# The front of a transformer-block kernel: five columns of x in exchanged blocks, squares from the blocks, first weights in four groups, rstd transposes inside the last column

## The chip, the cores and the metric

The kernel runs on one core of one Trainium2 chip. The metric is the time of one execution in device microseconds. TensorE is PE here (PEld is its weight load), VectorE DVE, ScalarE ACT, GpSimd POOL, SyncE SP. A line such as L2218 is a line of the kernel before.

## The reference

A whole block of an encoder on x of 1024 x 1024 floats: RMS norm, one combined projection, two kinds of attention, output projection, norm, residual, and a squared-ReLU MLP.

```
def rmsnorm(x, g):
    y = xf * lax.rsqrt(jnp.mean(xf * xf, axis=-1, keepdims=True) + EPS)
    return (y * g.astype(jnp.float32)).astype(x.dtype)
...
    h = rmsnorm(x, g_pre_mix[l])
    proj = jnp.einsum('bsd,de->bse', h, w_in[l]) + b_in[l]
    aq, ak, av, bq, bk, bv = jnp.split(proj, splits, axis=-1)
    out_a = mixer_a(aq, ak, av, sinks[l], t5_bias)
    out_b = mixer_b(bq, bk, bv, rel_table[l])
    y = jnp.einsum('bse,ed->bsd', jnp.concatenate([out_a, out_b], axis=-1), w_out[l])
    x = x + rmsnorm(y, g_post_mix[l])
    u = jnp.square(jax.nn.relu(jnp.einsum('bsd,df->bsf', rmsnorm(x, g_pre_mlp[l]), w_up[l])))
    x = x + rmsnorm(jnp.einsum('bsf,fd->bsd', u, w_down[l]), g_post_mlp[l])
```

The change touches the first norm and the first pieces of the projection only.

## The kernel before, in words

**Number form.** Every operand of a large product is split into a high part rounded to fp32r and a low part, the rest; a product is three matmuls: high by high, high by low, low by high. So each operand costs a rounding copy on ACT (`x_hi`, `w1_hi`, `wv_hi`) and a subtraction on DVE (`x_lo`, `w1_lo`, `wv_lo`).

**The front.** x is taken in eight columns k of 128 features by 1024 rows. The norm's factor g1 is put on with the rounding; the row factor rstd is put on later, on the products. For the projection the features must lie on the partitions, so each column is turned. Columns 0 to 4 are loaded as rows (`xraw`) and turned by PE, eight 128x128 transposes per column into PSUM banks 6 and 7 (`x_transposes`, L2230); there ACT reads them for `x_hi` (L1115) and DVE for `x_lo` (L1542). Columns 5 to 7 (`EXCHANGED`) are loaded by four DMAs each with their 32x32 blocks already in exchanged places (`x_blocks`, L693, in pieces of 128 bytes); a STREAM_TRANSPOSE on DVE, which turns within 32x32 blocks, then gives the column (`x_turned`, L1549). Of a column PE makes the products with three tiles of first weights, e in the order 2, 0, 1, each in two halves of 512 rows, with three matmuls of 128x512 for each: 18 per column, summed in PSUM over the columns (`first_products`, L2218 to L2220).

**The row norm.** ACT squares rows of `xraw` (columns 0 to 4, 128x640, L1090) and of a second copy of columns 5 to 7 as rows (`x_rows`, 128x384, L1092), eight each, and accumulates each over its row; DVE adds the two halves (L1556), ACT takes the root (L1122), DVE makes rstd, DVE and ACT lay it out in columns (`rcols`, L1562, L1126), PE turns these by eight transposes (L2290) ahead of column 7, and ACT copies the result out of PSUM (`rrow`, L1142).

**The value products.** Next PE makes value products for row tiles 0 and 1, over all eight k, two halves each; those of tile 0 wait for rrow and, at each k, for `wv_lo` k (L1521). While they run, DVE scales the first tiles by rrow (`tile_scaled`, L1582), ACT rounds them (L1136), DVE takes their low part (`tile_lo`, L1595).

**What sets the order.** Every engine's program is written out by hand, as loops over k with waits on semaphores; an engine runs its own list strictly in order. Tables shape it: `SQUARED` says behind which column's rounding ACT squares which rows, `SPLIT_WITH` which first weights it rounds there, `VALUES_WITH` which value weights DVE handles between the scaled tiles. All big loads go out on SP's queue in written order. POOL makes bias rows, and then issues nine small loads of constants (L980 to L987) behind a wait for column 6. Two of the waits matter later on: ACT's copy of value weights 5 waits for DVE's scaling of the query biases (`s_bsc`, L1568), and the fill weights on SP's queue (L726) for the last squares.

Of the kernel before, what the change touches and what calls it, by code (L numbers as in the profile page):

```python
# [50 lines left out]
SQUARED = ((), (), (), (0, 1, 2, 3), (4, 5, 6), (7, 8, 9, 10, 11), (12, 13, 14, 15), ())  # L51
# [145 lines left out]
EXCHANGED = (5, 6, 7)  # L197
# [3 lines left out]
SPLIT_WITH = ((), (1,), (2,), (3,), (4, 5), (6, 7), (), ())  # L201
# [4 lines left out]
def column_done(k):  # L206

    return 2 * (k + 1) if k < 2 else k + 3

# [50 lines left out]
def build(nc, x, w_in, b_in, w_out, sinks, t5, rel, g_pre_mix, g_post_mix, g_pre_mlp, g_post_mlp,  # L260
# [11 lines left out]
    with ctx:  # L272
# [32 lines left out]
        x_rows = sb("x_rows", 188, [P, T, KT - KX, P])  # L305
# [4 lines left out]
        sq = sb("sq", 150.25, [P, 2, KX, P])  # L310
        wv_hi = [sb(f"wv_hi{k}", at, [P, VW], F32R) for k, at in enumerate((84, 86.5, 89, 91.5, 94, 96.5, 116, 118.5))]
# [3 lines left out]
        x_blocks = {k: sb(f"x_blocks{k}", at, [P, SEQ]) for k, at in zip(EXCHANGED, (92, 76, 108))}  # L315
        x_turned = {k: sb(f"x_turned{k}", at, [P, SEQ]) for k, at in zip(EXCHANGED, (112, 116, 76))}
# [82 lines left out]
        def blocks_landed(k):  # L399
            return {5: (s_xb, 64), 6: (s_g1, 16 + 64), 7: (s_x0, 16 + 64)}[k]  # L400
# [3 lines left out]

        def load_first_weights(eng, g):
            k0, k1 = ((0, 1), (1, 3), (3, KT))[g]
            eng.dma_start(w1_raw[:, k0:k1, 0:P], w_in[AK, :, k0:k1, :]).then_inc(s_w1[g], 16)
            for hh in range(2):
                if g == 0:
                    eng.dma_start(w1_raw[:, 0, P:3 * P].rearrange("p (a n) -> p a n", a=2)[:, :, 64 * hh:64 * hh + 64],  # L410
                                  w_in[2 * hh, :, 0].rearrange("p (a n) -> p a n", a=2)).then_inc(s_w1[g], 16)
                else:
                    for p in range(2):
                        at = P + P * p + 64 * hh
                        eng.dma_start(w1_raw[:, k0:k1, at:at + 64], w_in[2 * hh, :, k0:k1, 64 * p:64 * p + 64]  # L415
                                      ).then_inc(s_w1[g], 16)
# [89 lines left out]
        s_g1 = sem("g1_landed")  # L506
# [5 lines left out]
        s_id = sem("ones_then_ident_ready")  # L512
# [14 lines left out]
        s_ss1 = sem("sumsq_halves_added")  # L527
# [152 lines left out]
        def _(sp):  # L680
# [2042 lines left out]
```

## Time and profile before

| what | us |
|---|---|
| median of 3 runs | 1035.18 (1034.83 to 1035.95) |
| the profiled execution | 1036.56 |
| its span | 1034.3 |
| PE busy in it | 1023.8 (99%) |
| DVE busy | 765.0 |
| ACT busy | 471.2 |
| POOL busy | 217.6 |

The profiled execution is a single run, 1.38 us above the median of the others; 2.3 us of it lie outside the span. The granted TensorE clock was 0.999 of full speed. A timeline row gives the start in the span, the busy time, engine, line, operation and tile, how many instructions were put together, and, in brackets, how long the engine had been idle before and on what. Starts of neighbouring instructions overlap a little, so the distance between two starts is often under the busy time. A row of windows gives a stretch and its length, then busy time and count of PE, PEld, DVE, ACT and POOL in it, then the granted clock, the busy share of the DMA engines and what they moved.

### The profile page before, as it was taken

To read this page: it belongs to the slowest core of one execution; us is meant where nothing else is said; L and a number is where in the kernel's file an instruction comes from. 1 tells how busy PE (TensorE), PEld (TensorE's weight loads), DVE (VectorE), ACT (ScalarE), POOL (GpSimd) and SP (SyncE) were. 2 spreads that over 40 slices of the span, in tenths; PEclk is the share of its full clock that TensorE was granted. 3 is DMA by queue.
4 is the path that set the end of the run, shared out by engine and by line. 5 is a ranking of instruction groups with operands and counts; after the bars stand their busy time and mean duration, and the time that the engine had idled before them with its cause. 6 is when DMAs were issued, how large, how long until landed. Compare 5 with 4: busy or idle time off the path is not lost.

```text
span 1034.3 us, 15804 instructions
## 1 busy us (share of the span) xinstructions
PE 1023.8 (99%) x5531; PEld 851.2 (82%) x5531; DVE 765.0 (74%) x1498; ACT 471.2 (46%) x989; POOL 217.6 (21%) x213
## 2 busy tenths in 40 slices
PE   8999999999999999999999999999999999999997
PEld 7899887778777888888888888888888888888886
DVE  3854678866689478888988788786454777778997
ACT  5732355554478477846131221221354444444562
POOL 4100000000000003148675675671100000000000
PEclk9999999999999999999999999999999999999999
DMA  9944442110061475145444434446777733454344
GB/s 212 238 130 120 119 130 64 63 49 22 27 202 65 122 174 153 41 132 214 163 173 162 164 132 153 163 141 215 246 244 238 239 98 96 138 196 142 95 138 168
DMA packets 133007, 149.50 MB, mean 145 GB/s; under 512 B 68136, under 2 KB 83376, under 8 KB 130880
## 3 DMA queue, kind: packets, MB, share of 16 engines
q1 hardware_dynamic: 131856, 148.25, 46.3%
q8 instruction: 45, 0.74, 0.3%
q14 instruction: 34, 0.28, 0.1%
q10 hardware_dynamic: 688, 0.20, 0.1%
q0 software_dynamic: 384, 0.04, 0.1%
HBM read 105.22 MB, written 47.49 MB: 148 GB/s over the span
## 4 chain that ended last, share of the span: by engine, by line
PE 94%; SPq 3%; issue 1%; DVE 1%; ACT 1%; DMA 0%; DVEq 0%; ACTq 0%
PE ps L2218 27%; PE ps L2220 27%; PE ps L2219 27%; PE ps L2431 3%; PE ps L2417 3%; PE ps L2398 2%; SPq L693 1%; PE ps L2342 1%; PE ps L2377 1%; PE ps L2550 1%; PE ps L2552 1%; PE ps L2538 1%; SPq L415 1%; PE ps L2568 0%; SPq L684 0%
## 5 line engine op out<-in xcount | busy, mean ns | idle before, releaser
L2219 PE MATMUL ps<-tm_lo,sm_hi 128*128 128x512 f32 (+1 forms) x450 | 174.6, 388 | 0.0
L2220 PE MATMUL ps<-tm_hi,sm_lo 128*128 128x512 f32 (+1 forms) x450 | 174.6, 388 | 0.0
L2218 PE MATMUL ps<-tm_hi,sm_hi 128*128 128x512 f32 (+1 forms) x450 | 174.6, 388 | 0.0
L2218 PE MATMUL ps<-b_hi,wc_hi 128*128 128x512 f32 x448 | 174.6, 390 | 0.0
L2220 PE MATMUL ps<-b_hi,wc_lo 128*128 128x512 f32 x448 | 174.3, 389 | 0.0
L2219 PE MATMUL ps<-b_lo,wc_hi 128*128 128x512 f32 x448 | 174.3, 389 | 0.0
L1475 ACT ACTIVATE sm_hi<-sm_raw 128x512 fp32r<-128x512 f32 x112 | 70.7, 631 | 162.1 <-DMA sm_raw<-u_matrices 162.1
L2122 DVE TENSOR_TENSOR sm_lo<-sm_raw,sm_hi 128x512 fp32r<-128x512 f32 x112 | 77.5, 692 | 78.4 <-ACT sm_hi L1475 77.7
L2219 PEld LDWEIGHTS ps<-tm_lo,sm_hi 128*128 128x128 f32 x450 | 84.5, 188 | 17.6
L2218 PEld LDWEIGHTS ps<-tm_hi,sm_hi 128*128 128x128 f32 x450 | 84.5, 188 | 17.4
L2218 PEld LDWEIGHTS ps<-b_hi,wc_hi 128*128 128x128 f32 x448 | 84.1, 188 | 17.8 <-DVE wc_lo L1894 0.3
L2220 PEld LDWEIGHTS ps<-tm_hi,sm_lo 128*128 128x128 f32 x450 | 84.5, 188 | 17.3
L2220 PEld LDWEIGHTS ps<-b_hi,wc_lo 128*128 128x128 f32 x448 | 84.1, 188 | 17.7
L2219 PEld LDWEIGHTS ps<-b_lo,wc_hi 128*128 128x128 f32 x448 | 84.1, 188 | 17.2
L1387 ACT ACTIVATE p1s<-ps 128x512 f32<-128x512 f32 x16 | 9.6, 598 | 181.1 <-PE ps L2220 175.5
L2124 DVE TENSOR_TENSOR tm_lo<-w,tm_hi 128x512 fp32r<-128x512 f32 x112 | 76.6, 684 | 0.0
L1894 DVE TENSOR_TENSOR wc_lo<-up_raw,wc_hi 128x512 fp32r<-128x512 f32 x48 | 56.6, 1202 | 19.6 <-ACT wc_hi L1327 19.6
L1894 DVE TENSOR_TENSOR wc_lo<-wc_raw,wc_hi 128x512 fp32r<-128x512 f32 x64 | 68.9, 1079 | 2.5 <-POOL wc_raw L1036 2.5
L1484 ACT ACTIVATE tm_hi<-w 128x512 fp32r<-128x512 f32 x112 | 69.0, 616 | 0.0
L1028 POOL TENSOR_TENSOR wc_raw<-up_raw 128x512 f32<-128x512 f32 x16 | 22.4, 1401 | 221.4 <-DVE small L673 138.6
L2218 PE MATMUL ps<-x_hi,wf_hi 128*128 128x512 f32 x160 | 66.7, 417 | 0.0
L2220 PE MATMUL ps<-x_hi,wf_lo 128*128 128x512 f32 x160 | 62.8, 392 | 0.0
(256 smaller groups left out, 2057.5 us busy)
## 6 DMA issues: line engine op xcount, KB each, us to landing
u_matrices<-stage SPq DMA_DIRECT2D x112, 256.0 KB, 2.0
sm_raw<-u_matrices SPq DMA_DIRECT2D x112, 256.0 KB, 2.7
up_raw<-in_w_up SPq DMA_DIRECT2D x16, 1024.0 KB, 5.1
w<-in_w_down SPq DMA_DIRECT2D x64, 256.0 KB, 4.2
w_raw<-in_w_in SPq DMA_DIRECT2D x8, 512.0 KB, 3.5
xr<-in_x SPq DMA_DIRECT2D x8, 512.0 KB, 4.8
x_rows<-xr SPq DMA_DIRECT2D x8, 512.0 KB, 5.5
xf<-x_rows SPq DMA_DIRECT2D x8, 512.0 KB, 3.6
```

The costliest lines, as they stand in the source:

```text
L1028: nc.gpsimd.tensor_tensor(wc_raw[s][5][:], a21, a22, ALU.add).then_inc(s_wsum, 1)
L1475: nc.scalar.activation(sm_hi[r][:], sm_raw[r][:], ACT.Copy).then_inc(s_shi, 1)
L1484: nc.scalar.activation(tm_hi[r][:], down_weights[q][c][:], ACT.Copy).then_inc(s_thi, 1)
L1894: nc.vector.tensor_tensor(wc_lo[s][p][:], src, wc_hi[s][p][:].bitcast(F32), ALU.subtract).then_inc(s_wlo[s], 1)
L2122: nc.vector.tensor_tensor(sm_lo[r][:], sm_raw[r][:], sm_hi[r][:].bitcast(F32), ALU.subtract).then_inc(s_slo, 1)
L2124: nc.vector.tensor_tensor(tm_lo[r][:], down_weights[q][c][:], tm_hi[r][:].bitcast(F32), ALU.subtract).then_inc(s_tlo, 1)
L2218: pe.matmul(out, w_hi_, x_hi_, start=start, stop=False)
L2219: pe.matmul(out, w_hi_, x_lo_, start=False, stop=False)
L2220: return pe.matmul(out, w_lo_, x_hi_, start=False, stop=stop)
L2398: last = pe.matmul(score_of(n, hh)[:, c * width:(c + 1) * width], q[rows, tok], k[rows, keys], start=(i == 0), stop=(i == 2))
L2417: last = pe.transpose(ps[:, bank, i * P:(i + 1) * P], prob_of(n, hh)[:, c0 + k * P:c0 + (k + 1) * P], ident[:])
L2431: last = pe.matmul(ps[64 * hh:64 * hh + 64, 7, (t % 4) * P:(t % 4) * P + P], v_tok[:, t + 1 - nk + k, at + 64 * hh:at + 64 * hh + 64], pro ...
```

## The change

- Columns 3 and 4 are now loaded as exchanged blocks too and turned by DVE; PE turns columns 0 to 2 only. `x_rows` is gone.
- The squares of columns 0 to 2 come from rows as before (eight of 128x384). Those of columns 3 to 7 are taken by ACT on the blocks (`square_blocks`, 128x1024 each) into three buffers. POOL adds those of columns 4, 5 and 6 to those of 3. DVE sums that buffer and the squares of column 7 over the 32 elements of each block (`tensor_reduce`), adds both, PE adds over the partitions with a matrix `sel` of zeros and ones (`add_squares`, 128x32, behind e = 2 of column 6), and DVE puts the result on `ss1` in four small additions.
- The first weights come in four groups instead of three; SP waits for the first x_hi and x_lo before the last of them.
- The row transposes stand behind e = 2 of column 7 instead of ahead of column 7.
- In DVE's list the order at columns 3 to 7 is different, ACT's value copies 0 and 1 stand ahead of the root, and DVE's scaling of the query biases stands behind the first two scaled tiles.
- POOL's nine small loads stand behind its additions instead of behind a wait for column 6.

The diff, cut to its core:

```diff
-SQUARED = ((), (), (), (0, 1, 2, 3), (4, 5, 6), (7, 8, 9, 10, 11), (12, 13, 14, 15), ())
+SQUARED = ((), (), (0, 1, 2, 3, 4, 5), (6, 7), (), (), (), ())
...
-EXCHANGED = (5, 6, 7)
+FIRST_GROUPS = ((0, 1), (1, 3), (3, 5), (5, KT))
+EXCHANGED = (3, 4, 5, 6, 7)
...
-SPLIT_WITH = ((), (1,), (2,), (3,), (4, 5), (6, 7), (), ())
+SPLIT_WITH = ((), (1,), (2,), (3, 4), (5,), (6,), (7,), ())
...
+def blocks_squared(k):
+    return rows_squared(k) + k - EXCHANGED[0] + 1
...
-            load_x(0)
...
-            load_x_blocks(7)
+            for k in range(KT):
+                if k in EXCHANGED:
+                    load_x_blocks(k)
+                else:
+                    load_x(k)
+                if k in (1, 3):
+                    load_first_weights(sp, (k + 1) // 2)
+                elif k == 4:
+                    sp.wait_ge(s_xhi, 1)
+                    sp.wait_ge(s_xlo, 1)
+                    load_first_weights(sp, 3)
...
-            pool.wait_ge(s_xt, column_done(KT - 2))
+            for k in EXCHANGED[1:-1]:
+                pool.wait_ge(s_sq, blocks_squared(k))
+                if k > EXCHANGED[1]:
+                    pool.wait_ge(s_part, k - EXCHANGED[1])
+                nc.gpsimd.tensor_tensor(sq_blocks[0][:], sq_blocks[0][:], squares_of(k)[:], ALU.add).then_inc(s_part, 1)
             pool.dma_start(g2, g_pre_mlp).then_inc(s_const, 16)
...
+            def square_blocks(k):
+                act.wait_ge(*blocks_landed(k))
+                n = k - EXCHANGED[0]
+                if n >= 3:
+                    act.wait_ge(s_part, n - 2)
+                nc.scalar.activation(squares_of(k)[:], x_blocks[k][:], ACT.Square).then_inc(s_sq, 1)
...
+                    if k > 4:
+                        square_blocks(k)
                     act.wait_ge(s_xt, column_done(k))
                     nc.scalar.activation(x_hi[:, k], column(k), ACT.Copy, scale=g1[:, k:k + 1]).then_inc(s_xhi, 1)
                 for j in SPLIT_WITH[k]:
                     first_hi(j)
+                if EXCHANGED[0] <= k <= 4:
+                    square_blocks(k)
                 for n in SQUARED[k]:
                     square_rows(n)
-                if k == KT - 2:
-                    act.wait_ge(s_ss1, 1)
+                if k == KT - 1:
+                    for j in range(2):
+                        value_hi(j)
+                    act.wait_ge(s_ss1, 5)
                     nc.scalar.activation(std1, ss1, ACT.Sqrt, bias=epsc, scale=1.0 / D).then_inc(s_std1, 1)
...
+                    if k in EXCHANGED and k <= 6:
+                        turn_blocks(k)
+                    if EXCHANGED[0] < k < KT - 1:
+                        first_lo(k)
+                    if k == 6:
+                        turn_blocks(k + 1)
+                    if k == KT - 1:
+                        dve.wait_ge(s_part, len(EXCHANGED) - 2)
+                        nc.vector.tensor_reduce(out=parts[:, 0], in_=sq_blocks[0][:].rearrange("p (c i) -> p c i", i=32),
+                                                axis=mybir.AxisListType.X, op=ALU.add).then_inc(s_ss1, 1)
...
                     dve.wait_ge(s_xhi, column_done(k))
...
+            dve.wait_ge(s_const, 192)
+            nc.vector.tensor_scalar(bcol[:, 1:9], bcol[:, 1:9], -SCALE, None, ALU.mult).then_inc(s_bsc, 1)
...
+            def add_squares():
+                pe.wait_ge(s_xlo, column_done(EXCHANGED[0] - 1))
+                pe.wait_ge(s_id, 9)
+                pe.wait_ge(s_ss1, 3)
+                pe.matmul(ps[:, 6, 0:32], sel[:], parts[:, 2], start=True, stop=True).then_inc(s_ss1, 1)
...
+                    if e == 2 and k == KT - 2:
+                        add_squares()
+                    elif e == 2 and k == KT - 1:
+                        row_transposes()
...
-                elif k == KT - 1:
-                    pe.wait_ge(s_xlo, column_done(EXCHANGED[0] - 1))
-                    pe.wait_ge(s_rcol, 2)
```

DVE's list at columns 6 and 7, as it was (`small` at L1556 is the sum of the two halves of the squares):

```order
L1549 STREAM_TRANSPOSE x_turned_131<-x_blocks_128 128x1024 [waits g1_landed]
L1526 TENSOR_TENSOR w_lo<-w_raw,w_hi 128x384 [waits first_weights_hi_ready]
L1553 STREAM_TRANSPOSE bv_rows<-bv_cols 128x32 [waits const_landed]
L1542 SCALAR_TENSOR_TENSOR x_lo<-x_turned_131,small,x_hi 128x1024 [waits x_hi_ready]
L1549 STREAM_TRANSPOSE x_turned_132<-x_blocks_129 128x1024 [waits first_column_second_half_then_last_blocks_landed]
L1526 TENSOR_TENSOR w_lo<-w_raw,w_hi 128x384 [waits first_weights_hi_ready]
L1556 TENSOR_TENSOR small<-small 128x8 [waits squares_ready]
```

And DVE's list from the turn of column 6 to x_lo of column 7, as it is after the change (`sq_blocks_104` holds the added squares, `sq_blocks_106` those of column 7):

```order
L1563 STREAM_TRANSPOSE x_turned_139<-x_blocks_134 128x1024 [waits x_columns_or_blocks_then_wo_landed6]
L1555 TENSOR_TENSOR w_lo<-w_raw,w_hi 128x384 [waits first_weights_hi_ready]
L1563 STREAM_TRANSPOSE x_turned_140<-x_blocks_135 128x1024 [waits x_columns_transposed,squares_ready,x_columns_or_blocks_then_wo_landed7]
L1593 SCALAR_TENSOR_TENSOR x_lo<-x_turned_139,small,x_hi 128x1024 [waits x_hi_ready]
L1585 TENSOR_REDUCE parts<-sq_blocks_104 128x32 [waits block_squares_added]
L1588 TENSOR_REDUCE parts<-sq_blocks_106 128x32 [waits squares_ready]
L1591 TENSOR_TENSOR parts<-parts 128x32 [waits block_sums_reduced_added_multiplied_then_sumsq_ready]
L1593 SCALAR_TENSOR_TENSOR x_lo<-x_turned_140,small,x_hi 128x1024 [waits x_hi_ready]
```

The turn of column 7 now stands ahead of x_lo of column 6, and both reductions ahead of x_lo of column 7.

POOL's list where the constants' loads begin, before:

```order
L974 TENSOR_SCALAR brow<-relrow 8x384
L976 TENSOR_SCALAR brow<-relrow 8x384
L980 DMA small<-in_g_pre_mlp 128x8 [waits x_columns_transposed]
L981 DMA small<-in_sinks 128x8
L983 DMA small<-in_b_in 64x2
```

The same place of POOL's list after the change:

```order
L996 TENSOR_SCALAR brow<-relrow 8x384
L998 TENSOR_SCALAR brow<-relrow 8x384
L1005 TENSOR_TENSOR sq_blocks_104<-sq_blocks_104,sq_blocks_105 128x1024 [waits squares_ready]
L1005 TENSOR_TENSOR sq_blocks_104<-sq_blocks_104,sq_blocks_106 128x1024 [waits block_squares_added,squares_ready]
L1005 TENSOR_TENSOR sq_blocks_104<-sq_blocks_104,sq_blocks_105 128x1024 [waits block_squares_added,squares_ready]
L1006 DMA small<-in_g_pre_mlp 128x8
L1007 DMA small<-in_sinks 128x8
```

Three additions with two SBUF inputs each stand where the wait for column 6 stood.

DVE's list where the value products begin (`small` at L1568 and L1569 are the query biases and the sinks), before:

```order
L1521 TENSOR_TENSOR wv_lo_123<-wv_raw_115,wv_hi_107 128x640 [waits value_weights_hi_ready]
L1568 TENSOR_SCALAR small<-small 128x8 [waits const_landed]
L1569 TENSOR_SCALAR small<-small 128x8
L1582 SCALAR_TENSOR_TENSOR tmp<-ps,rrow 128x512 [waits first_halves_done,rstd_rows_copied]
L1582 SCALAR_TENSOR_TENSOR tmp<-ps,rrow 128x512 [waits first_halves_done]
L1521 TENSOR_TENSOR wv_lo_124<-wv_raw_116,wv_hi_108 128x640 [waits value_weights_hi_ready]
```

The same place after the change:

```order
L1550 TENSOR_TENSOR wv_lo_127<-wv_raw_119,wv_hi_111 128x640 [waits value_weights_hi_ready]
L1630 SCALAR_TENSOR_TENSOR tmp<-ps,rrow 128x512 [waits first_halves_done,rstd_rows_copied]
L1630 SCALAR_TENSOR_TENSOR tmp<-ps,rrow 128x512 [waits first_halves_done]
L1655 TENSOR_SCALAR small<-small 128x8 [waits const_landed]
L1656 TENSOR_SCALAR small<-small 128x8
L1550 TENSOR_TENSOR wv_lo_128<-wv_raw_120,wv_hi_112 128x640 [waits value_weights_hi_ready]
```

The two scaled tiles and the two small scalings have changed places; value copy 5 on ACT waits for the first of the small ones.

## Rows read from the trace of the kernel before

**Rows 1.** Windows: busy us and instructions per engine, clock, DMA share, GB/s.

```profile
0.00:45.40 45.40, 42.26 (x209) 35.27 (x210) 23.75 (x39) 29.67 (x63) 16.65 (x53) 1.00 0.97 223
45.40:100.00 54.60, 54.60 (x424) 53.36 (x423) 32.64 (x106) 18.41 (x54) 2.73 (x14) 1.00 0.52 143
```

**Rows 2.** Timeline of PE: column starts, row transposes, value products of tiles 0, 1.

```profile
17.27 1.03 PE L2230 MATMUL ps<-ident,xraw 128*128 128x128 f32 x8
...
27.25 0.39 PE L2218 MATMUL ps<-x_hi,w_hi 128*128 128x512 f32 x1
...
31.33 0.39 PE L2218 MATMUL ps<-x_hi,w_hi 128*128 128x512 f32 x1
...
36.05 0.50 PE L2218 MATMUL ps<-x_hi,w_hi 128*128 128x512 f32 x1 [0.49 <-DVE x_lo L1542]
...
40.39 1.06 PE L2290 MATMUL ps<-ident,rcols 128*128 128x128 f32 x8
...
45.42 0.30 PE L2218 MATMUL ps<-wv_hi,x_hi 128*128 128x320 f32 x1
...
52.45 0.31 PE L2218 MATMUL ps<-wv_hi,x_hi 128*128 128x320 f32 x1
```

**Rows 3.** Timeline of ACT, the front.

```profile
14.37 0.51 ACT L1101 ACTIVATE w_hi<-w_raw 128x384 fp32r<-128x384 f32 x1
...
28.73 0.92 ACT L1101 ACTIVATE w_hi<-w_raw 128x384 fp32r<-128x384 f32 x2
...
33.53 1.15 ACT L1115 ACTIVATE x_hi<-x_turned,small 128x1024 fp32r<-128x1024 f32 x1 [1.13 <-DVE x_turned L1549]
34.59 0.51 ACT L1092 ACTIVATE sq<-x_rows 128x384 f32<-128x384 f32 x1
...
38.96 1.29 ACT L1126 ACTIVATE rcols<-ones,small 128x128 f32<-128x128 f32 x4
...
41.49 1.03 ACT L1142 ACTIVATE rrow<-ps 128x1024 f32<-128x1024 f32 x1
42.42 1.98 ACT L1097 ACTIVATE wv_hi<-wv_raw 128x640 fp32r<-128x640 f32 x3
```

**Rows 4.** Timeline of DVE, the front and the start of the values.

```profile
35.92 1.24 DVE L1549 STREAM_TRANSPOSE x_turned<-x_blocks 128x1024 f32<-128x1024 f32 x1
37.08 0.52 DVE L1526 TENSOR_TENSOR w_lo<-w_raw,w_hi 128x384 fp32r<-128x384 f32 x1
37.52 0.16 DVE L1556 TENSOR_TENSOR small<-small 128x8 f32<-128x8 f32 x1
...
39.75 1.28 DVE L1542 SCALAR_TENSOR_TENSOR x_lo<-x_turned,small,x_hi 128x1024 fp32r<-128x1024 f32 x1
...
45.53 1.28 DVE L1582 SCALAR_TENSOR_TENSOR tmp<-ps,rrow 128x512 f32<-128x512 f32 x2
46.73 0.81 DVE L1521 TENSOR_TENSOR wv_lo<-wv_raw,wv_hi 128x640 fp32r<-128x640 f32 x1
47.47 0.74 DVE L1595 SCALAR_TENSOR_TENSOR aq_lo<-tmp,small,aq_hi 128x512 fp32r<-128x512 f32 x1
```

**Rows 5.** Timelines of POOL and DVE later: operations with two SBUF inputs.

```profile
521.11 1.73 POOL L1048 TENSOR_TENSOR stage<-stage,stage 128x512 f32<-128x512 f32 x1
...
526.21 1.29 POOL L1053 TENSOR_TENSOR stage<-stage,stage 128x512 f32<-128x512 f32 x1
...
511.07 0.68 DVE L1894 TENSOR_TENSOR wc_lo<-wc_raw,wc_hi 128x512 fp32r<-128x512 f32 x1
...
521.62 1.77 DVE L1894 TENSOR_TENSOR wc_lo<-wc_raw,wc_hi 128x512 fp32r<-128x512 f32 x1
```

**Rows 6.** Windows, columns as in rows 1: two stretches of loads.

```profile
31.00:33.00 2.00, 2.00 (x11) 1.65 (x10) 0.76 (x1) 1.40 (x6) 0.00 (x0) 1.00 1.09 170
9.00:12.00 3.00, 3.00 (x19) 2.56 (x18) 1.32 (x2) 1.68 (x3) 0.53 (x1) 1.00 1.10 282
```

**Rows 7.** Timeline of SP's queue: the four loads of block column 5.

```profile
15.22 6.51 SPq L693 DMA_DIRECT2D x_blocks<-in_x  x4
```

More of the change, by code:

```diff
@@ L208, in column_done, with rows_squared @@
     return 2 * (k + 1) if k < 2 else k + 3
+def rows_squared(k):
+    return sum(len(SQUARED[j]) for j in range(k))
+ROW_SQUARED = [n + 1 + max(0, k - EXCHANGED[0] + 1) for k in range(KT) for n in SQUARED[k]]
+def blocks_squared(k):
+    return rows_squared(k) + k - EXCHANGED[0] + 1
 def chunks_until(n):
@@ L780, in _ @@
             sp.wait_ge(s_rep, 16)
+            sp.wait_ge(s_ss1, 2)
             load_bias(0)
@@ L963, in _ @@
             nc.gpsimd.memset(bv_cols[:], 0.0).then_inc(s_id, 1)
+            nc.gpsimd.memset(sel[:], 0.0).then_inc(s_id, 1)
+            for a in range(4):
+                pool.wait_ge(s_id, 5 + a)
+                nc.gpsimd.affine_select(out=sel[:].rearrange("p (b i) -> p b i", i=32), in_=sel[:].rearrange("p (b i) -> p b i", i=32),
+                                        compare_op=ALU.not_equal, fill=1.0, base=-32 * a, pattern=[[0, 4], [-1, 32]],
+                                        channel_multiplier=1).then_inc(s_id, 1)
             pool.wait_ge(s_xt, 2)
@@ L1137, in tile_hi @@
                                      bias=bias_of(e)).then_inc(s_ehi, 1)
-            for k in range(2):
-                value_hi(k)
             act.wait_ge(s_rowp, 1)
@@ L1553, in _ @@
                     nc.vector.transpose(bv_rows[:], bv_cols[:]).then_inc(s_bv, 1)
-                elif k == KT - 2:
-                    dve.wait_ge(s_sq, 2 * T)
-                    nc.vector.tensor_tensor(ss1, ss1, ya1, ALU.add).then_inc(s_ss1, 1)
+                elif k == KT - 1:
+                    dve.wait_ge(s_ss1, 4)
+                    for q in range(4):
+                        rows = slice(32 * q, 32 * q + 32)
+                        last = nc.vector.tensor_tensor(ss1[rows], ss1[rows], ps[rows, 6, 0:32].rearrange("p (t q) -> p q t", q=4)[:, q],
+                                                       ALU.add)
+                    last.then_inc(s_ss1, 1)
+                    first_lo(k)
                     dve.wait_ge(s_std1, 1)
@@ L2233, in x_transposes, with row_transposes @@
                 last.then_inc(s_xt, 1)
+            def add_squares():
[3 more added lines that the diff above has]
+                pe.matmul(ps[:, 6, 0:32], sel[:], parts[:, 2], start=True, stop=True).then_inc(s_ss1, 1)
+            def row_transposes():
+                pe.wait_ge(s_rcol, 2)
+                for t in range(T):
+                    last = pe.transpose(two(6)[:, t * P:(t + 1) * P], rcols[:, t * P:(t + 1) * P], ident[:])
+                last.then_inc(s_rowp, 1)
             def first_products(k):
@@ L2285, in _ @@
                     x_transposes(k + 1)
-                elif k == KT - 1:
-                    pe.wait_ge(s_xlo, column_done(EXCHANGED[0] - 1))
-                    pe.wait_ge(s_rcol, 2)
-                    for t in range(T):
-                        last = pe.transpose(two(6)[:, t * P:(t + 1) * P], rcols[:, t * P:(t + 1) * P], ident[:])
-                    last.then_inc(s_rowp, 1)
                 first_products(k)
```

96 lines of the change are left out of this document (41 added, 55 removed).

## The prediction

> **What bounds the kernel now.** I read the stages first. After 45.4 us TensorE is the bound: in 45.4 to 100 it is busy for all of 54.60 us [rows 1]. So whatever the front does to the moment at which the value products start, 45.42 [rows 2], goes one to one into the span. In the front PE is busy for 42.26 of 45.40 us [rows 1]. Then I read PE's timeline from 17.27, where the change's first effect on it falls. A column that carries the transposes of the next one takes 4.99 us (17.27 to 27.25, two of them), one without 4.08 (27.25 to 31.33). Column 6 waits 0.49 for x_lo. From 40.39 the row transposes and column 7 take 5.03, so the transposes cost 0.95. From 17.27 to 45.42 this is 28.15 us. The value products then take 45.42 to 52.45 for eight k, 0.88 each [rows 2].
>
> **What PE gains.** Two sets of eight transposes, those of columns 3 and 4, go: 2 x (4.99 - 4.08) = 1.82. Added is one 128x32 matmul for the block sums. No such shape is in the trace; between a 128x128 transpose (0.95 / 8 = 0.12) and a 128x512 matmul (0.39) I take 0.27, with its weights. Without any wait PE would need 6 x 4.08 + 0.92 + 0.27 = 25.67 from 17.27, and start the values at 42.94: **-2.5 us**. The rest asks whether the other engines keep up with that.
>
> **ACT.** Removed: 16 row squares and their accumulator reads; added: eight of 128x384 and five of 128x1024. A row of 128x384 takes 0.51 in the trace; a 128x1024 square I price as x_hi from the same kind of buffer, 1.06 from its start to the next (33.53 to 34.59) [rows 3]. From the weight copy at 14.37, over at 14.8: six rows to 17.9, x_hi(3) 18.9, two weight copies (0.92 for the pair, with some overlap) 19.75, square 3 20.8, two rows 21.8, x_hi(4) and a copy, and square 4 ends at 24.7. None of it makes PE wait: columns 3 and 4 are due at 21.35 and 25.43. But 24.7 is the start of what does.
>
> **POOL and DVE, the term that decides.** POOL now adds the squares of blocks 4, 5 and 6 into one buffer, three TENSOR_TENSOR of 128x1024 with two SBUF inputs. The trace has 128x512 ones only: 1.29 us alone, 1.73 when a DVE operation is in the way. Beside such an add a DVE operation with two SBUF inputs goes from 0.68 to 1.77: it began at 521.62 inside POOL's add (521.11 to 522.84) and ended 0.55 after it [rows 5]. So the two take turns and do not overlap. A 128x1024 add is then 2 x 1.29 = 2.58 at most, and 2.38 if 0.2 of each is start-up; I take 2.5. On DVE the operations with two SBUF inputs are first_lo (0.52, and 0.44 to the next start, 37.08 to 37.52) and x_lo on a turned column (1.28, by the same overlap 1.2); the turns have one input (1.24) [rows 4]. In turns:
> - add 4 runs 24.8 to 27.3; first_lo(5), ready meanwhile, 27.3 to 27.75;
> - add 5 27.75 to 30.2; x_lo(5) to 31.4;
> - add 6 31.4 to 33.8; first_lo(6) to 34.25; turn(7), which stands ahead of x_lo(6) in the new order, to 35.5; x_lo(6) to 36.7;
> - two TENSOR_REDUCEs of 128x1024. The trace has none; the nearest rows are a turn (1.24) and x_lo (1.28), and half of that is the lower end; I take 1.25 each: 37.8 and 39.0, the parts added at 39.2.
>
> Each of them is on the path of PE. Column 5 could start at 29.5 and gets x_lo(5) at 31.4: **+1.95**. Column 6 could then start at 35.5 and gets x_lo(6) at 36.7: **+1.2**. The block-sum matmul stands behind its first third, reached at 38.1, and waits until 39.25: **+1.15**. Behind that matmul stand all later matmuls of columns 6 and 7. That puts the start of the values at 42.94 + 4.3 = 47.25.
>
> By the Trainium skill, page "GPSIMD Engine Reference", section "3.1 Elementwise — side-by-side cycle accounting", a POOL add of 2048 elements takes 4497 ns, so about 2.25 us for 1024 as an estimate; three adds would give back 0.75 and the sum would end near +2.3. The trace's 1.29 for 512 elements lies above that pace, and no run here shows the larger add.
>
> **Row norm.** After the parts comes x_lo(7) (to 40.4), four adds of 128x8 size (0.16 each, 40.8 [rows 4]), sqrt, rstd and the columns. In the trace the chain from the sum of squares at 37.52 to the last rcols at 38.96 + 1.29 takes 2.73 [rows 3, 4], so they stand at about 43.45. PE reaches the row transposes, now behind the first third of column 7, at 43.6. Hidden, by 0.15 only: an extra 1 us there costs 0.85.
>
> **Value stage.** Before, rrow is copied at 41.49 to 42.5, 2.9 ahead of the values. After, the row transposes end at 44.5 and rrow at 45.7, 1.5 ahead. ACT's value copies 2 to 4 stand behind rrow (1.98 for three [rows 3]) and DVE's subtractions behind those (0.81 for one, less the overlap 0.77 [rows 4]): 48.7. Then two tile scalings (1.28), and only now the scaling of the query biases, 49.95, on which ACT's value copy 5 waits. Behind it come copy 5, subtraction 5 (51.6), a tile's low part (0.74), a scaling (0.69) and subtraction 6, ready at 53.75. PE wants it at 47.25 + 6 x 0.88 = 52.5: **+1.25**. This is no matter of the starting moment: rrow and values move together.
>
> **Transfers.** x_rows (2 x 768 KB) goes; columns 3 and 4 come in 128-byte pieces. Where nearly only such pieces moved the trace shows 170 GB/s (31 to 33), against 282 in 9 to 12 [rows 6]. A column of 0.524 MB at 170 is 3.1 us. With the order on SP's queue I get blocks 3 to 7 landed at about 15, 20, 25, 28.5 and 31.5, against needs of 16.6, 20.8, 26.5, 29.5 and 33.5: covered by 1 to 2 us. The four weight groups are due at 23.2 and land near 22. POOL's nine small loads go out behind add 6, from 33.8, and their results are wanted at 49.9, 16 us later: nothing.
>
> **The sum.** -2.5 + 1.95 + 1.2 + 1.15 + 1.25 = **+3.05 us**. The profiled execution took 1036.56 with a span of 1034.3; it would become 1039.6 (span 1037.35). The median of the three runs lies 1.38 below the profiled one, so on its scale 1035.18 + 3.05 = **1038.2**. Bounds: adds of 2.38 or 2.58, +2.7 to +3.3; reduces at half price, -1.1 of wait; the block-sum matmul 0.12 or 0.5, -0.15 or +0.2; row norm 0.85 over. Together +1.7 to +4.1.
>
> **Rivals.**
> - *A, the adds cost DVE nothing* (the turns are not taken with 128x1024 adds, or fall so that DVE's are done first). Then the adds follow one another, 24.8 + 3 x 2.5 = 32.3, reduces 32.3 to 36 with turn(7) between, and only the block sums make PE wait, 1.1; with 1.25 in the value stage -2.5 + 1.1 + 1.25 = -0.15: 1035.0. For it: the rows show adds half as large only. Against: in those the turns are plain [rows 5].
> - *B, nothing waits.* The reduces at half price and the value stage fed in time by other wakes: -2.5, 1032.7. For it speaks that PE had only one wait of 0.49 in this stretch [rows 2]; against it that three separate waits have to vanish.
> - *C, slower: the blocks land late.* The four loads of x_blocks took 6.51 us of SP's queue in the trace [rows 7], twice the 3.1 I count, though partly behind other loads. With 1 us more per column block 7 lands at about 35.8, turn(7) ends at 37, x_lo(6) behind it 38.2, the parts 40.9 and the block sums with them: 1.7 later than the forecast, +4.8, 1040.0. It decides once block 7 is later than about 34.2. At 6.51 per column it would be +14, but a queue that stands behind half-megabyte loads issues slowly without the pieces being slow, so I leave that out. The Trainium skill, page "DMA: Bandwidth & Descriptors", section "Specifications", says that pieces under 512 B miss the line rate since each is read, changed and written; by that rule the change goes the wrong way, and the 170 against 282 GB/s agrees.
>
> **How the numbers follow.** Forecast 0.48, A 0.26, B 0.10, C 0.16. A measurement of this kernel tells about 0.2% (2.1 us) from no change. Of the forecast's 0.48 some 0.09 lies under +2.1; nearly all of A is within. Faster 0.11 (B, an edge of A), same 0.34, slower 0.55. The range leaves out B and an edge of A below, and the worse half of C above: 1034.0 to 1041.5. Its likeliest case alone is 1036.9 to 1039.3.
>
> **What would show it.** Right: PE waits at the first matmuls of columns 5 and 6 for x_lo, and at the 128x32 matmul for the parts; POOL's adds at 2.4 to 3 us each, and DVE's first_lo(5) and x_lo(5) stretched beyond 0.52 and 1.28 while one is in flight; a PE wait in the value products at k = 6 for wv_lo. Column pace 4.08 for columns 2 to 4. A: x_lo(5) at its 1.28 and columns 5 and 6 without a wait. C: PE's waits end with a turn that itself waited for a block's landing. Wrong altogether: the values starting before 43.5, or a PE gap after 60 us that was not there.

## The result, and the profile after

| | before | after |
|---|---|---|
| median us | 1035.39 (6 runs) | 1040.03 (6 runs, 1039.52 to 1040.55) |
| the profiled execution, its span | 1036.56, 1034.3 | 1039.52, 1037.7 |

The ratio is 1.0044, 95% interval 1.0031 to 1.0057: 4.6 us slower, 3.2 to 5.9 by the interval. The first view is what PE waited for from 10 to 60 us of the changed kernel (engine, tile and line, releaser; total, times, longest):

```profile
PE ps L2269 <- DVE x_lo L1593: 2.0, 1, 2.0
PE ps L2269 <- DVE wv_lo L1550: 1.0, 1, 1.0
PE ps L2290 <- DVE parts L1591: 0.3, 1, 0.3
```

And its PE timeline, the rows that answer to [rows 2]:

```profile
31.29 0.79 PE L2269 MATMUL ps<-x_hi,w_hi 128*128 128x512 f32 x1 [2.02 <-DVE x_lo L1593]
...
38.85 0.38 PE L2290 MATMUL ps<-parts,sel 128*128 128x32 f32 x2 [0.26 <-DVE parts L1591]
...
43.28 1.06 PE L2295 MATMUL ps<-ident,rcols 128*128 128x128 f32 x8
...
46.94 0.30 PE L2269 MATMUL ps<-wv_hi,x_hi 128*128 128x320 f32 x1
...
53.63 0.41 PE L2269 MATMUL ps<-wv_hi,x_hi 128*128 128x320 f32 x1 [1.04 <-DVE wv_lo L1550]
...
55.49 0.31 PE L2269 MATMUL ps<-wv_hi,x_hi 128*128 128x320 f32 x1
...
465.59 0.50 PE L2269 MATMUL ps<-b_hi,wc_hi 128*128 128x512 f32 x1 [0.37 <-DVE wc_lo L1945]
```

Columns 2 to 4 now follow each other without a gap. Then PE waits for x_lo of column 5 (31.29), a little for the block sums (38.85), and at k = 6 of the value products (53.63). The values start at 46.94 instead of 45.42, 1.52 later. Their first eight k end at 55.49 instead of the 52.45 of [rows 2]: another 1.52, of which 1.04 is the idle time in the brackets; the rest lies around that wait, in starts that follow each other less closely. The last 0.4 of the 3.4 between the two spans is a wait at 465.59 that the profile of the kernel before does not have. Why the values start late shows in DVE's timeline from the turn of column 5 to the parts:

```profile
26.22 1.25 DVE L1563 STREAM_TRANSPOSE x_turned<-x_blocks 128x1024 f32<-128x1024 f32 x1 [1.79 <-DMA x_blocks<-in_x]
27.39 0.52 DVE L1555 TENSOR_TENSOR w_lo<-w_raw,w_hi 128x384 fp32r<-128x384 f32 x1
28.69 2.55 DVE L1593 SCALAR_TENSOR_TENSOR x_lo<-x_turned,small,x_hi 128x1024 fp32r<-128x1024 f32 x1 [0.79 <-ACT x_hi L1143]
31.16 0.20 DVE L1600 STREAM_TRANSPOSE bv_rows<-bv_cols 128x32 f32<-128x32 f32 x1
31.29 1.20 DVE L1563 STREAM_TRANSPOSE x_turned<-x_blocks 128x1024 f32<-128x1024 f32 x1
32.42 1.49 DVE L1555 TENSOR_TENSOR w_lo<-w_raw,w_hi 128x384 fp32r<-128x384 f32 x1
33.83 1.23 DVE L1563 STREAM_TRANSPOSE x_turned<-x_blocks 128x1024 f32<-128x1024 f32 x1
34.99 1.24 DVE L1593 SCALAR_TENSOR_TENSOR x_lo<-x_turned,small,x_hi 128x1024 fp32r<-128x1024 f32 x1
36.15 1.21 DVE L1585 TENSOR_REDUCE parts<-sq_blocks 128x32 f32<-128x1024 f32 x1
37.28 1.20 DVE L1588 TENSOR_REDUCE parts<-sq_blocks 128x32 f32<-128x1024 f32 x1
38.52 0.19 DVE L1591 TENSOR_TENSOR parts<-parts 128x32 f32<-128x32 f32 x1
```

The turn of column 5 waited 1.79 us for its block to land. From 28.69 on DVE has no pause, and two of its operations are stretched: x_lo of column 5 takes 2.55 instead of the 1.28 of [rows 4], the low weights of column 6 take 1.49 instead of 0.52. Both fall into POOL's additions. The low weights of column 5 (27.39) lie inside an addition too and keep their 0.52; there it is the addition that is longer, 2.80 instead of 2.40 (POOL's timeline):

```profile
24.56 2.40 POOL L1005 TENSOR_TENSOR sq_blocks<-sq_blocks,sq_blocks 128x1024 f32<-128x1024 f32 x1 [1.17 <-ACT sq_blocks L1119]
27.36 2.80 POOL L1005 TENSOR_TENSOR sq_blocks<-sq_blocks,sq_blocks 128x1024 f32<-128x1024 f32 x1 [0.40 <-ACT sq_blocks L1119]
30.74 2.75 POOL L1005 TENSOR_TENSOR sq_blocks<-sq_blocks,sq_blocks 128x1024 f32<-128x1024 f32 x1 [0.58 <-ACT sq_blocks L1119]
```

Windows of the changed kernel (columns as in rows 1) show one thing that was not in the forecast: behind the gap of 2.02 us the granted clock stands at the lower of its two levels, 1.2 GHz.

```profile
29.30:31.30 2.00, 0.01 (x1) 0.01 (x1) 2.00 (x3) 1.06 (x1) 1.42 (x2) 0.99 1.14 178
...
33.30:34.30 1.00, 1.00 (x4) 0.81 (x3) 1.00 (x2) 1.00 (x3) 1.00 (x3) 0.50 1.11 325
...
35.30:36.30 1.00, 1.00 (x6) 0.83 (x5) 1.00 (x2) 1.00 (x2) 1.00 (x3) 1.00 1.19 301
```

From 31.29 PE needed 7.30 us for the 24 matmuls up to the block sums; at the pace of 4.08 per 18 it would have been 5.44.

### The profile page after: what moved, and what is told of

Read it like the earlier page. It is cut to its first block, busy times and chain, and to the rows that moved or that the text cites. A ratio compares the mean times of both kernels' runs of the same rounds, so it can differ in the third digit from the quotient of the medians.

```text
span 1037.7 us, 15793 instructions
## 1 busy us (share of the span) xinstructions
PE 1024.6 (99%) x5517; PEld 850.9 (82%) x5517; DVE 772.4 (74%) x1506; ACT 470.7 (45%) x978; POOL 229.0 (22%) x221
## 4 chain that ended last, share of the span: by engine, by line
PE 89%; DVE 4%; issue 2%; SPq 2%; ACT 1%; DMA 1%; POOL 0%; DVEq 0%; ACTq 0%
PE ps L2269 26%; PE ps L2271 25%; PE ps L2270 25%; PE ps L2492 2%; PE ps L2478 2%; PE ps L2459 2%; PE ps L2403 1%; SPq L719 1%; DVE wc_lo L1945 1%; PE ps L2438 1%; PE ps L2611 1%; PE ps L2613 1%; PE ps L2599 1%; SPq L441 1%; DMA up_raw<-in_w_up 1%
```

## The experiments

All are edits of the changed kernel unless said otherwise. "Values" is the time at which PE starts the value products.

**1. POOL's additions away.**

```diff
-                nc.gpsimd.tensor_tensor(sq_blocks[0][:], sq_blocks[0][:], squares_of(k)[:], ALU.add).then_inc(s_part, 1)
+                nc.gpsimd.tensor_scalar(sq_blocks[0][:, 0:8], squares_of(k)[:, 0:8], 1.0, None, ALU.mult).then_inc(s_part, 1)
```

> POOL's three additions of 128x1024 squares are replaced by three one-input operations of 128x8, so the squares of columns 4 to 6 are left out of the row norm (apart from eight elements of each row of blocks). Everything else stays as in the changed kernel. Theory (POOL's additions take turns with DVE's two-input operations, and DVE, without a pause from x_lo of column 5 on, sets the block sums): x_lo of column 5 falls from 2.55 to 1.28 us and ends near 29.95, the first weights' low part of column 6 falls from 1.49 to 0.5, the wait of PE at column 5 falls from 2.02 to about 0.8, the parts are ready near 37.2 instead of 38.7, and the value products start near 45.4 instead of 46.94: 1.5 us less. Rival (the landings of the blocks set all of it): the DVE durations shorten, the turns wait for landings instead, and the values start within 0.4 of 46.94.

Measured: 1039.0 us, ratio 1.0033 (1.0020 to 1.0045), values at 46.95. DVE's timeline of this kernel:

```profile
26.88 1.25 DVE L1563 STREAM_TRANSPOSE x_turned<-x_blocks 128x1024 f32<-128x1024 f32 x1 [2.85 <-DMA x_blocks<-in_x]
...
29.34 1.28 DVE L1593 SCALAR_TENSOR_TENSOR x_lo<-x_turned,small,x_hi 128x1024 fp32r<-128x1024 f32 x1 [0.78 <-ACT x_hi L1143]
...
31.80 0.52 DVE L1555 TENSOR_TENSOR w_lo<-w_raw,w_hi 128x384 fp32r<-128x384 f32 x1
33.80 1.25 DVE L1563 STREAM_TRANSPOSE x_turned<-x_blocks 128x1024 f32<-128x1024 f32 x1 [1.49 <-DMA x_blocks<-in_x]
```

The stretching is gone (1.28, 0.52): it was the additions. But the time won is spent waiting for block 7, which landed at 33.8 here (32.35 in the changed kernel's profile), and the parts come at 38.5 as before. The theory fell as far as the additions alone were to set the end. The profile shows the slowest of the six executions, though: their median is 1.0 us below the changed kernel's, and all six (1038.34 to 1039.50) lie below its six. So the additions alone do cost something, less than the 1.5 expected.

**2. PE kept busy in the gap.**

```diff
             for k in range(1, KT):
...
+                if k == 5:
+                    for _ in range(19):
+                        pe.transpose(ps[:, 7, 0:P], ident[:], ident[:])
                 first_products(k)
```

> The changed kernel with 19 transposes of the identity into a free PSUM bank ahead of column 5, so that PE is busy in the gap of 2.02 us. In the changed kernel the granted clock was 0.50 from 31.3 to 34.3 behind that gap, and the 24 matmuls up to the block sums took 7.30 us instead of 24 x 0.227 = 5.44. Theory (the block sums end on DVE at 38.7 whatever PE does before): the clock stays at 1.00, the 1.86 us come back as waits, about 0.9 at column 6 and 1.1 at the block sums, and the values start within 0.3 of 46.94. Rival (the low clock is on the path): the values start 1.5 to 1.9 us sooner.

Measured: 1039.66 us, ratio 1.0040 (1.0025 to 1.0055). PE's timeline:

```profile
29.07 2.23 PE L2355 MATMUL ps<-ident 128*128 128x128 f32 x19
31.89 0.50 PE L2269 MATMUL ps<-x_hi,w_hi 128*128 128x512 f32 x1 [0.58 <-DVE x_lo L1593]
...
36.89 0.50 PE L2269 MATMUL ps<-x_hi,w_hi 128*128 128x512 f32 x1 [0.59 <-DVE x_lo L1593]
...
39.47 0.38 PE L2290 MATMUL ps<-parts,sel 128*128 128x32 f32 x2 [0.91 <-DVE parts L1591]
```

The clock stays up (1.00 from 31.9 to 36.9 us), and what it gives back is spent in the two waits of the forecast, at column 6 and at the block sums. Block 5 landed 0.6 later here (turn at 26.81), and the block sums stand 0.6 later: in this profile the low clock cost nothing. The median is 0.4 below the changed kernel's, with executions of both in the same range.

**3. The query biases first.** The three lines of the scaling are put back ahead of `dve.wait_ge(s_row, 1)`.

> The changed kernel with DVE's scaling of query biases and sinks ahead of the first two scaled tiles, as it stood before the change. Theory (ACT's value copy 5 waits for it and the chain behind it feeds the value products at k = 6): the scaling is done near 48.4 instead of 49.7, PE's wait of 1.04 at the low value weights in the value products goes, and everything behind comes about 1.0 to 1.3 us sooner; the start of the values stays at 46.94. Rival (value copies 2 to 4 behind rrow are what is late): the wait stays above 0.6.

Measured: 1039.23 us, ratio 1.0038 (1.0023 to 1.0053). In what PE waited for, 1.04 became:

```profile
PE ps L2269 <- DVE wv_lo L1550: 0.4, 1, 0.4
```

So 0.6 of the 1.04 of idle time was the moved scaling. The eight k took 7.73 us (48.44 to 56.17) after 8.55 in the changed kernel and 7.03 before, so it is 0.8 of the 1.52 lost there, and the median is 0.8 lower as well. The rest I put down to rrow being ready so shortly ahead of the values; no run with five columns tests that, but the wait is 0.34 in run 11 and gone in run 12, which take value copies ahead of rrow. In this profile block 5 landed at 27.7 and the values started at 48.4, so the start itself has to be read from the landing (below).

**4. x_lo of column 6 ahead of the turn of column 7.**

> The changed kernel with x_lo of column 6 ahead of the turn of column 7 on DVE. Theory (DVE's sum of work up to the parts is what counts, not its order): x_lo of column 6 ends about 1.1 us sooner, near 35.1, and gains nothing, the parts stay within 0.3 of 38.7 and the values within 0.3 of 46.94. Rival (x_lo of column 6 is on PE's path, as forecast with a wait of 1.2): the values start about 1 us sooner.

Measured: 1040.45 us, ratio 1.0051 (1.0036 to 1.0066). Turn of column 5 at 27.00, parts at 39.28, values at 47.70, which is 20.70 after the turn where the changed kernel took 20.72: the order made no difference to the end.

Runs 2 to 4 and the changed kernel agree in one number. From the turn of column 5 to the start of the parts they took 39.13 - 26.81, 40.02 - 27.69, 39.28 - 27.00 and 38.52 - 26.22: 12.28 to 12.33 us each, whatever PE did. Each such execution starts this chain when block 5 lands, and that moved between 26.2 and 27.7.

**5 and 6. Wide pieces, with and without the additions.**

```diff
-                rows = x[:, k * P:(k + 1) * P].rearrange("(c j) (a i) -> a j c i", j=32, i=32)
+                rows = x[:, k * P:(k + 1) * P].rearrange("(t p) n -> p t n", p=P)
...
-                    sp.dma_start(x_blocks[k][32 * a:32 * a + 32].rearrange("j (c i) -> j c i", i=32), rows[a]
+                    sp.dma_start(x_blocks[k][:].rearrange("p (t n) -> p t n", n=P)[:, 2 * a:2 * a + 2], rows[:, 2 * a:2 * a + 2]
```

Both read the five columns in plain order, without the exchange of blocks; the second also leaves the squares of columns 4 to 6 out, by the edit of run 1. Each load now fills 128 partitions instead of 32, so the size of the pieces is not the only thing that changes.

> The changed kernel with the five block columns read in pieces of 512 bytes instead of 128 (the same bytes into the same buffers by the same number of loads, but rows in plain order: x of columns 3 to 7 is thereby wrong). At the 282 GB/s of the earlier loads instead of 170 a column of 0.524 MB takes 1.9 us instead of 3.1, so block 5 lands near 22.6 and block 7 near 26.5 (26.2 and 32.4 in the changed kernel, up to 27.7 and 33.8 in the runs since). Theory of two chains of about the same length (landing of the blocks, and POOL's additions in turn with DVE): the additions still follow one another, x_lo of column 5 and the low weights of 6 are still stretched, the parts are ready near 38 and the values start between 46.0 and 47.0 (46.94 in the changed kernel). Rival (the landings alone set the front): the values start before 44.5.

> Both taken away at once: blocks in pieces of 512 bytes (columns 3 to 7 of x wrong) and POOL's three additions replaced by operations of 128x8 (the squares of columns 4 to 6 left out). Taking the additions away alone left the start of the values at 46.95. Theory of two chains: now neither holds, DVE has the parts ready near 34.4, PE reaches the block sums at about 34.6 without a wait, and the values start between 42.6 and 43.5, some 4 us sooner, with the wait of about 1 us at k = 6 still there. Rival (something else in the new front, such as the row norm behind the block sums or ACT's order, is as late): the values start after 45.

Measured: 1038.26 us, ratio 1.0029 (1.0018 to 1.0041), and 1034.86 us, ratio 0.9993 (0.9984 to 1.0002). DVE's timeline of the first, and PE's of the second:

```profile
24.63 1.86 DVE L1555 TENSOR_TENSOR w_lo<-w_raw,w_hi 128x384 fp32r<-128x384 f32 x1
26.42 3.42 DVE L1593 SCALAR_TENSOR_TENSOR x_lo<-x_turned,small,x_hi 128x1024 fp32r<-128x1024 f32 x1
```

```profile
34.31 0.30 PE L2290 MATMUL ps<-parts,sel 128*128 128x32 f32 x2
...
42.28 0.30 PE L2269 MATMUL ps<-wv_hi,x_hi 128*128 128x320 f32 x1
```

| values start at | pieces of 128 bytes | of 512 bytes |
|---|---|---|
| with POOL's additions | 46.94 | 45.54 |
| without | 46.95 | 42.28 |

In these profiles each cost alone hides for the most part behind the other; together they are 4.66 us. The fronts do not begin alike: column 2 starts at 16.87, 16.89 (additions away), 16.39 (wide) and 16.63 (both). From there to the values it takes 30.07, 30.06, 29.15 and 25.65 us. The medians say the same less sharply: 1040.0, 1039.0, 1038.3 and 1034.9, so the two changes alone give 1.0 and 1.8, and together 5.2. With neither cost, PE has no wait between column 2 and the values, and its own gain of the forecast stands there. The start of the first was 0.5 better than expected (45.54 against 46.0 to 47.0), as much as its front was earlier.

**7. DVE reduces the squares itself.** POOL's additions go; the whole computation stays.

```diff
+            def reduce_squares(k):
+                dve.wait_ge(s_sq, blocks_squared(k))
+                nc.vector.tensor_reduce(out=parts[:, k - EXCHANGED[0]], in_=squares_of(k)[:].rearrange("p (c i) -> p c i", i=32),
+                                        axis=mybir.AxisListType.X, op=ALU.add).then_inc(s_part, 1)
...
```

> The changed kernel's whole computation without POOL's additions: DVE reduces the squares of each block column by itself (1.2 us each, those of columns 3 and 4 in its idle time ahead of the turn of column 5, that of column 5 ahead of x_lo of column 6), one small reduction adds the five parts, and x_lo of column 6 stands ahead of the turn of column 7. POOL's small loads keep their time. Theory: from the landing of block 5 to the parts DVE needs about 10.9 us instead of the 12.3 of the four kernels with additions; with block 5 landed at 26.2 to 27.0 the parts are ready at 37.1 to 37.9, and the values start 0.8 to 1.5 sooner than in a run with the additions and the same landing (landing of block 5 + 20.7). Rival (reductions cost DVE what the turns with POOL did): still landing + 20.7.

Measured: 1039.14 us, ratio 1.0043 (1.0028 to 1.0058). Turn of column 5 at 26.59, parts complete for PE at 38.39, values at 46.47, that is the turn + 19.9 instead of + 20.7. Gained 0.8, the lower end of what was expected: three more reductions of 1.15 eat most of what the turns with POOL had cost. The median is 0.9 below the changed kernel's. Most of PE's wait in the front now stands at one place, with 0.70 left at column 5; the wait in the value products grew to 1.46:

```profile
38.39 0.38 PE L2293 MATMUL ps<-parts,sel 128*128 128x32 f32 x2 [2.25 <-DVE parts L1591]
```

**8. Four exchanged columns.** Columns 4 to 7, reductions on DVE, biases first.

> One part of the change undone, and the two costs found taken out: four exchanged columns (4 to 7) instead of five, so PE turns column 3 again (0.91 us of PE) and one column less comes in small pieces; DVE reduces the squares itself as in the run above; the query biases are scaled ahead of the first tiles. Theory: block 5 lands about 1.2 us sooner, near 25.3, column 5 starts without a wait near 29.7, the parts are ready near 36.5 and the values start between 44.3 and 45.0, against 45.42 before the change and 46.94 with it; the wait at k = 6 is 0.4 or less. The time comes out between 1034.5 and 1036, about that of the kernel before. Rival (small pieces are not what makes the blocks late): the values start after 46.

Measured: 1038.11 us, ratio 1.0032 (1.0020 to 1.0043); slower than expected by 2 us. Its profile is of an execution of 1041.5 and not good for numbers; it shows ACT's row squares ahead of x_hi of column 4, and a wait of 2.20 at the block sums. Block 5 landed at 24.95, as the theory had it (25.3), so in this execution the blocks are not what was late.

**9. The kernel before, once more.**

> The kernel before the change once more, for a second profile: the first was taken of an execution of 1036.56 us, 1.38 above the median, and the changed kernel's of one 0.5 below its median, so that the two spans differ by 3.4 us and the medians by 4.6. Theory: the executions of the kernel before differ in its front, by the landing of the blocks, and a profile at the median time starts the values about 1 us before 45.42 and has no wait of 0.49 at column 6. Rival: the front is the same, values within 0.3 of 45.42, and the difference lies elsewhere in the span.

Measured: 1035.9 us, ratio 1.0004 (0.9995 to 1.0013); this profile is of an execution of 1036.29, and PE's timeline begins its first turned column earlier:

```profile
6.00 0.66 PE L2230 MATMUL ps<-ident,xraw 128*128 128x128 f32 x4 [0.72 <-DMA xraw<-in_x]
...
35.30 0.50 PE L2218 MATMUL ps<-x_hi,w_hi 128*128 128x512 f32 x1 [0.49 <-DVE x_lo L1542]
...
44.65 0.30 PE L2218 MATMUL ps<-wv_hi,x_hi 128*128 128x320 f32 x1
```

The values start 0.77 sooner than 45.42, all of it from the first landing (6.00 instead of 6.75); the wait at column 6 is the same, so that part of the theory was wrong. But its span is only 0.3 shorter: PE lost 0.4 of the 0.77 again between 100 and 147 us. So the front explains a part only of why these profiles are long. Spans of 73 timed executions of the kernel before lie at 32.6 to 34.3 above 1000, with three beyond (34.7, 35.6, 36.2) and 33.3 in the middle; both of its profiles (34.3 and 34.0) lie high. Those of the changed kernel go from 1037.7 to 1038.8, with 1038.2 in the middle, and its profile is the lowest. That is why the two profiles differ by 3.4 and the medians by 4.6. The time outside the span works the other way: 2.2 us before, 1.8 after.

**10. Three exchanged columns with squares from the blocks.**

> Only columns 5 to 7 exchanged, as before the change, with the changed kernel's squares from the blocks, so no second copy of these columns as rows; no additions on POOL, DVE reduces the three squares itself; x_lo of column 6 ahead of the turn of column 7, the query biases scaled ahead of the first tiles, the row transposes inside column 7. PE makes all transposes again. Theory: without 1.5 MB of rows block 7 lands near 30, the parts are ready near 35, PE waits nowhere between columns 2 and the values at k = 6, and the values start at 44.3 to 44.9, against 45.42 and 46.94; faster than the kernel before by 0.3 to 1 us. Rival (in the kernel before nothing of these loads was on the path but the 0.49): within 0.3 us of it.

Measured: 1038.86 us, ratio 1.0030 (1.0019 to 1.0042), values at 47.18: far from what was expected. Block 7 landed at 29.7 as foreseen, but nothing was ready for it. ACT's timeline and DVE's:

```profile
27.32 1.05 ACT L1115 ACTIVATE sq_blocks<-x_blocks 128x1024 f32<-128x1024 f32 x1
28.27 1.14 ACT L1139 ACTIVATE x_hi<-x_turned,small 128x1024 fp32r<-128x1024 f32 x1
```

```profile
29.44 1.28 DVE L1591 SCALAR_TENSOR_TENSOR x_lo<-x_turned,small,x_hi 128x1024 fp32r<-128x1024 f32 x1 [1.66 <-ACT x_hi L1139]
...
35.13 1.24 DVE L1564 STREAM_TRANSPOSE x_turned<-x_blocks 128x1024 f32<-128x1024 f32 x1
36.29 2.31 DVE L1556 TENSOR_REDUCE parts<-sq_blocks 128x32 f32<-128x1024 f32 x2
```

The square of block 5 now stands ahead of x_hi of column 5 on ACT, and the row squares ahead of both; DVE starts late and never catches up. The transposes are back on PE, there are few small pieces and no additions, and still this kernel is 3.3 us slower than the one before. The trace points to the way of the squares; but the weight groups, DVE's order and the place of the row transposes are those of the change too, so the squares alone are not shown to be the cause.

**11 and 12. Four columns, block sums later.** In the first, the block sums stand behind column 6, the row transposes two thirds into column 7, value copies 0 to 3 ahead of the root, the row squares spread; in the second, two more moves:

```diff
+                    first_lo(k)
                     dve.wait_ge(s_ss1, 4)
...
-                    first_lo(k)
                     dve.wait_ge(s_std1, 1)
...
+            value_hi(4)
             act.wait_ge(s_rowp, 1)
```

> Columns 4 to 7 exchanged, no additions on POOL, DVE reduces the squares of each block column, the block sums behind column 6 instead of inside it, the row transposes two thirds into column 7, the query biases scaled ahead of the first tiles, value copies 0 to 3 ahead of the root on ACT, and the row squares spread so that ACT has x_hi of column 4 ready sooner than in the other kernel with four columns. Theory: PE waits for the row columns at most 1 us, the parts are ready near 37, and the values start at 43.7 to 44.7; between 0.5 and 1.5 us faster than the kernel before. Rival (the landing of the blocks moves the parts to 38 or later, and the chain of 6.8 us from the parts to rrow ends behind column 7): the values start after 45, no faster than before.

> The kernel of v2_four with two moves: the low part of the first weights of column 7 stands ahead of DVE's additions of the block sums (in v2_four PE waited 1.46 us for it at column 7, because those additions wait for the matmul behind column 6), and value copy 4 stands ahead of rrow on ACT. Theory: column 7 starts at 38.5 instead of 40.0, PE waits at most 0.5 us for the row columns, the values start near 44.0 instead of 45.15 and the wait of 0.34 at k = 6 goes: 1.2 to 1.5 us faster than v2_four (1036.4 against 1035.6 of the kernel before), so 1034.9 to 1035.3, between equal and 0.07% faster than the kernel before. Rival (the row norm, now later than PE, takes what column 7 gains): the values start after 44.8 and the kernel stays slower than before.

Measured: 1036.4 us, ratio 1.0011 (1.0002 to 1.0020), values at 45.15, with a wait of 1.46 at column 7 for low weights that stood behind the block sums on DVE (a mistake of mine in the order): 0.8 us slower than the kernel before, where 0.5 to 1.5 faster was expected. Then 1035.12 us, ratio 0.9994 (0.9985 to 1.0003). PE's timeline of the second:

```profile
38.01 0.30 PE L2291 MATMUL ps<-parts,sel 128*128 128x32 f32 x2
...
41.66 1.09 PE L2296 MATMUL ps<-ident,rcols 128*128 128x128 f32 x8 [0.25 <-ACT rcols L1153]
...
43.99 0.31 PE L2270 MATMUL ps<-wv_hi,x_hi 128*128 128x320 f32 x1
```

It is 4.9 us faster than the changed kernel and cannot be told from the kernel before.

## Why the prediction was right, and where it was not

Forecast were +3.05 us and 1038.2; measured were +4.6 and 1040.0. Direction and mechanism hold; the size was too small by a third. Step by step:

- **PE's gain of 2.5** is there: in run 6, with nothing in the way, PE takes 25.65 us from column 2 to the values (16.63 to 42.28), where the forecast had 25.67. The block-sum matmul took 0.22 (39.07 - 38.85) for the 0.27.
- **Additions in turn with DVE.** Right in place and price: 2.40 to 2.80 us for the 2.5, x_lo(5) and first_lo(6) stretched, and run 1 shows that the additions do it. First_lo(5), which was to be stretched, was not. Half of the 4497 ns that the Trainium skill ("GPSIMD Engine Reference", section "3.1 Elementwise — side-by-side cycle accounting") states for 2048 elements was the estimate of 2.25; the undisturbed addition of 1024 took 2.40, and the measurement decides.
- **Reductions** at 1.25 were 1.20 and 1.21.
- **Column 5:** 1.95 forecast, 2.02 measured. **Column 6** and the **block sums:** 1.2 and 1.15 forecast, 0 and 0.26 measured, but 1.86 lost to the lower clock between them. The three add up to 4.14 against 4.3, since all of them wait in the end for the same parts. Run 2 turned the clock's loss back into the two waits. That x_lo(5) ended at 31.24 where 31.4 was forecast is luck in part: the forecast counted from POOL's first addition at 24.8, while DVE had stood idle for 1.79 us and POOL for 0.40 until block 5 landed and was squared.
- **Row norm hidden by 0.15:** by 0.09; the last columns were ready at 43.19 (41.91 + 1.28) and PE came at 43.28.
- **Value stage:** 1.25 forecast, 1.52 measured, of which 1.04 is PE's idle time before k = 6; the moved scaling is 0.8 of it (run 3).
- **Transfers: the step that failed.** "Covered by 1 to 2 us" was wrong. Blocks 5 and 7 landed at 26.2 and 32.4 instead of 25 and 31.5, and in other executions up to 27.7 and 33.8. Between 23 and 32 us the changed kernel moved 157 GB/s, not 170. So the turn of column 5 waits, and DVE's 12.3 us begin there. Rival C had this mechanism and the price 1040.0; what I had as an alternative came on top of the forecast, each hiding part of the other. That its price is the measured time is luck: block 7 landed before the 34.2 from which C was to decide. The rule of the Trainium skill on small pieces ("DMA: Bandwidth & Descriptors", section "Specifications") spoke against the change and the runs go the same way: with 512-byte pieces the same bytes of block 5 landed at 22.1 instead of 26.2. That the size alone does it is not shown (run 5 also changes the partitions).
- **The sum on the two profiles** is nearly exact, by luck: the values start 1.52 later where 1.83 was forecast (47.25 - 45.42), the value stage costs 1.52 for 1.25, and 3.04 stands against 3.05. The 0.4 at 465.59 was not in the forecast. A PE gap after 60 us was one of the forecast's signs of being wrong altogether; this one is small, some of the other runs show it and some do not, and no run says where it comes from.
- **The base of the sum: the other step that failed.** The forecast took the span of one profiled execution of the kernel before, 1034.3. The median of 1035.39 less the 2.24 outside the span is 1033.15, so the base was 1.15 too long. The changed kernel's middle span, 1038.2, is 0.85 above the 1037.35 forecast (0.35 of it in its profile), and 0.4 less time lies outside the span: 1.15 + 0.85 - 0.4 is the 1.6 us missing in the sum. I had put the base down to a late first landing; run 9 had an early one and was still long, so that stays open. How much of the 0.85 is landings I can't say: those of the timed executions are not recorded.
- **The bounds** of the sum, +1.7 to +4.1, were too narrow (all of them at once give +1.45 to +4.35), and 1040.0 lies above the likeliest case. It is inside the range because this took in half of C.

Rivals A and B fell: A said that without a cost of the additions the front would be about even, and run 1 shows a front without that cost that is as late in its profile and 3.7 us slower than before in the median. B let nothing wait, and PE waits.

Open stays why block 5 lands up to 1.5 us apart between executions of nearly the same kernel; that was not tried. The traces show that much of the spread is there at the issue: in the six profiles with the small pieces and five columns, SP had issued the last of its four loads at 23.5 to 25.4, and it landed 2.1 to 3.1 us later.

## What to carry to other kernels

Two chains of about equal length hide each other: take away one and little moves, so test them together before calling either harmless. Work taken from the bound engine is only worth what the engines that inherit it can still hold; here 1.8 us of transposes went to DVE and the loads, and the last columns of rstd were ready 2.9 us later (43.19 instead of 40.25). An operation that the old form gave away (ACT's row sums while squaring) has to be priced when the form is given up.

## What I had not expected of the hardware

Behind a gap of 2.02 us PE's granted clock was 0.50 for some 3 us; behind the gaps of 1.39 and 1.22 of run 1 it stayed up. The length of the gap alone does not decide: behind 2.25 in run 7 it stayed up, behind 2.20 in run 8 it fell (windows of both below, columns as in rows 1). With a DVE operation ready at any time, POOL's additions stretched x_lo up to 3.42 us (run 5), 2.7 times its own 1.28. And an execution's first landing moves its whole front: 0.77 us between two profiles of one and the same kernel, of which 0.3 was left at the end of the span.

```profile
38.40:41.40 3.00, 3.00 (x14) 2.53 (x15) 2.83 (x11) 0.30 (x1) 0.00 (x0) 1.00 0.96 245
```

```profile
41.30:44.30 3.00, 3.00 (x9) 2.33 (x8) 2.79 (x16) 1.30 (x5) 0.00 (x0) 0.50 0.61 199
```
